# One inference step of a small RWKV-7 and pooling decoder: the prompt's group norm computed inside the sample stage, and TensorE's loops written out

## The chip, the cores and the metric

The kernel runs on one core of a Trainium2 chip. Its metric is the device time of that core in microseconds (us): the median of the runs shown. Five engines run their own instruction streams and meet at semaphores: PE (TensorE), DVE (VectorE), ACT (ScalarE), POOL (GpSimd) and SP (SyncE), which issues the DMAs. "PEld" in the profile is TensorE loading weights.

## What is computed

Two layers: RWKV-7 time mixing, then a pooling mixer, each followed by a feed-forward block. Both a prompt of 512 tokens and 8 sequences of 4 sample tokens go through them, all in float32. The part at issue is the end of the time mixing: the recurrence's output y is normalised within each head of 64 channels, gets a bonus, is gated and multiplied by `w_o`:

```python
S, y = wkv7_scan(wkv_prev, r_h, hd(decay), k_h, v_h, -kk, kk * a_h)
mu = jnp.mean(y, axis=-1, keepdims=True)
var = jnp.mean(jnp.square(y - mu), axis=-1, keepdims=True)
y = ((y - mu) * lax.rsqrt(var + GN_EPS)).reshape(B, T, D) * gn_w + gn_b
bonus = jnp.sum(r_h * k_h * r_k, axis=-1, keepdims=True) * v_h
g = jax.nn.sigmoid(xg @ g1) @ g2
out = ((y + bonus.reshape(B, T, D)) * g) @ w_o
x = x + out
h = rmsnorm(x, norm_ffn)
x = x + jnp.square(jax.nn.relu(h @ ffn_w1)) @ ffn_w2
```

## The kernel before

Activations lie with channels on partitions: 1024 channels are KT = 8 tiles of 128, and the free dimension holds T = 544 tokens, 512 of the prompt and 32 of the samples. `X` is the residual, `R` first r and then y, `V` first v and then the bonus, `GH` the hidden layer of the gate. The order of all work is written by hand. TensorE fills numbered "jobs"; job j writes PSUM banks 2(j mod 4) and 2(j mod 4)+1, so it waits until job j-4 has been emptied. ACT and DVE, each in its own written order, empty the jobs (`wait_filled`, `wait_emptied`).

The stages, in order: loading, the projections r, k, v, and then

- **tiles**: the prompt's recurrence in TILES = 4 tiles of 128 tokens. `pe_tile` (with `dve_tile`, `act_tile`, `pool_tile`) runs three times in a loop `Fori` on every engine and once more written out, as the last tile. A tile begins on TensorE with `Q0` to `Q3` (L655), which need the rates that DVE writes last (L1642), goes on with `M`, the products of the first square `P2` (L600), and ends with `YU` (L793).
- **sample stage** (`pe_samples`, `act_samples`, `dve_samples`): the 32 sample tokens. The states are transposed in (`s0t0` to `s0t3`, L561), then come `Q`, `M`, `P2`, `tBK`, `XT2`, `tV`, `bonus`, the 256 small products of `GY` (L879), `tG`, `U`, `YU`, and for four pairs of sequences the state sums `SS0` to `SS3` (L912, each added on DVE by L1798) and the transposes `TO0` to `TO3` (L561), whose copies SP stores.
- **group norm** for all 544 tokens, after the samples (`GN_JOBS`): for each of 8 tiles a `mean` (L1016, a product of 128 rows with `bmean`), one `var` (L1004: eight tiles summed into 16 rows), eight `gate` jobs (L1020 with 128 rows and L1021 with 32 rows of `g2`), and eight `spread` jobs (L1018: 16 rows of 1/std spread to 128 channels). Each job is two products of 272 columns. DVE subtracts the mean (L1950), takes the reciprocal (L1953), and then for each tile multiplies (L1960), adds the bonus (L1965) and gates (L1969); ACT makes the high part (L1383) and DVE the low part (L1972) of the result, which `w_o` needs.
- **w_o**: four units of weights of 256 columns, 384 products (L547), then the sums of squares of the norm (L575), and
- the first feed-forward block: CHUNKS = 4 passes of a loop on every engine (3072 products, L547); pooling; the second feed-forward block alike; the outputs.

A float32 product is two records in the trace; the large products are split into three products of a rounded type (`xs_hi`, `xs_lo`, `w_hi`, `w_lo`). `act_split` and `dve_split` make the two parts of a unit of weights, of which two buffers exist. The loops on TensorE are these, and the same `with` stands before both calls of `pe_ffn`:

```python
            with pe.Fori(0, TILES - 1) as i:
                pe_tile(pe, i)
            pe_tile(pe, TILES - 1, last=True)
```

## Time and profile before

| | |
|---|---|
| median of 3 runs (lowest to highest) | 1521.79 us (1521.44 to 1523.41) |
| the profiled execution | 1522.32 us, of which its span 1520.3 us |
| busy over the span: PE, PEld | 1438.9 us (95%), 1383.5 us (91%) |
| busy: DVE, ACT, POOL | 713.3 us (47%), 513.8 us (34%), 29.2 us (2%) |
| mean granted TensorE clock | 0.953 |
| DMA | 100.90 MB, 21.1% of the 16 engines' time on queue 1 |

The span runs from the first to the last instruction; a row's times are in it. "Busy" for PE is the union of modelled, overlapping products, so it says when PE had work, not how fast that work went. The granted clock is 1.00 at 2.4 GHz and 0.50 at 1.2 GHz. A group's mean covers one record; successive records overlap, so what a record costs in a row of them is the group's time over its count.

### The profile page before, as it was taken

Reading aid. Unit: us, or ns where it says so; the run is one execution under the profiler, and the core shown is the slowest. Engines: PE = TensorE matmul, PEld = TensorE weight load, DVE = VectorE, ACT = ScalarE, POOL = GpSimd, SP = SyncE. Lnnn points to the kernel's source line nnn. Section 1 sums busy time; section 2 is a strip of 40 time slices with the busy share of each in tenths; the row PEclk is TensorE's granted clock in tenths of the full one; section 3 lists DMA queues with packets and bytes.
Section 4 is the critical chain, followed back from the end, with each engine's and each line's share of the span. In section 5 each row is a group of like instructions: output and inputs, shape, how many; then the busy total and the mean of one; then the engine's idle time right before and its main releaser. Section 6 shows DMA issues by size and latency. Waiting matters only on the chain.

```text
span 1520.3 us, 33819 instructions
## 1 busy us (share of the span) xinstructions
PE 1438.9 (95%) x14990; PEld 1383.5 (91%) x14990; DVE 713.3 (47%) x859; ACT 513.8 (34%) x661; POOL 29.2 (2%) x28
## 2 busy tenths in 40 slices
PE   5899998898999889999999999999499999999998
PEld 4899998898989885899999999999389999999998
DVE  7746257585762423744334234343774233343332
ACT  5433236363543334333223132132153123131234
POOL 0000001010110000000000000000000000000000
PEclk7999999999999759799999999999799999999999
DMA  5123300000030014022222222221222322223211
GB/s 153 56 84 103 98 1 3 4 3 4 3 58 4 9 41 116 28 84 84 87 85 97 92 83 83 83 83 55 69 71 89 106 83 83 83 83 104 85 60 59
DMA packets 108887, 100.90 MB, mean 66 GB/s; under 512 B 21552, under 2 KB 106872, under 8 KB 108786
## 3 DMA queue, kind: packets, MB, share of 16 engines
q1 hardware_dynamic: 108786, 99.36, 21.1%
q8 instruction: 87, 1.43, 0.4%
q14 instruction: 14, 0.11, 0.0%
HBM read 94.18 MB, written 5.18 MB: 65 GB/s over the span
## 4 chain that ended last, share of the span: by engine, by line
PE 61%; DVE 3%; issue 1%; ACT 1%; DMA 0%; ACTq 0%; DVEq 0%
PE ps L547 54%; PE ps L575 1%; DVE pool_sum L2015 1%; PE ps L561 1%; PE ps L912 1%; PE ps L879 1%; PE ps L1021 1%; PE ps L1020 1%; PE ps L1016 1%; PE ps L1004 0%; DVE r_all L1965 0%; DVE r_all L1960 0%; DVE xs_lo L1972 0%; DMA pool_state_rows<-in_state_pool 0%; DVE pool_diff L2021 0%
## 5 line engine op out<-in xcount | busy, mean ns | idle before, releaser
L547 PE MATMUL ps<-xs_hi,w_hi 128*128 128x272 f32 (+1 forms) x2656 | 555.4, 290 | 16.6 <-DVE xs_lo L1904 8.6
L547 PE MATMUL ps<-xs_hi,w_lo 128*128 128x272 f32 (+1 forms) x2656 | 552.9, 290 | 0.0
L547 PE MATMUL ps<-xs_lo,w_hi 128*128 128x272 f32 (+1 forms) x2656 | 551.0, 289 | 0.0
L547 PEld LDWEIGHTS ps<-xs_hi,w_hi 128*128 128x128 f32 (+1 forms) x2656 | 420.0, 189 | 20.4 <-issue 11.1
L547 PEld LDWEIGHTS ps<-xs_lo,w_hi 128*128 128x128 f32 (+1 forms) x2656 | 419.5, 189 | 0.5
L547 PEld LDWEIGHTS ps<-xs_hi,w_lo 128*128 128x128 f32 (+1 forms) x2656 | 416.4, 189 | 0.5
L1471 DVE TENSOR_TENSOR w_lo<-w_raw,w_hi 128x2048 fp32r<-128x2048 f32 (+1 forms) x83 | 188.7, 2273 | 165.0 <-ACT w_hi L1122 164.4
L1122 ACT ACTIVATE w_hi<-w_raw 128x2048 fp32r<-128x2048 f32 (+1 forms) x83 | 157.0, 1891 | 291.4 <-PE ps L547 286.0
L1822 DVE TENSOR_TENSOR x_res<-x_res,ps 128x544 f32<-128x544 f32 x64 | 46.1, 720 | 207.4 <-PE ps L547 207.4
L1285 ACT ACTIVATE square_tmp<-relu_tmp 128x544 f32<-128x544 f32 x64 | 42.2, 659 | 268.1 <-DVE relu_tmp L1816 268.1
L1816 DVE SCALAR_TENSOR_TENSOR relu_tmp<-ps,rstd 128x544 f32<-128x544 f32 x64 | 46.3, 723 | 130.0 <-PE ps L547 130.0
L1828 DVE TENSOR_TENSOR xs_lo<-square_tmp,xs_hi 128x544 fp32r<-128x544 f32 x64 | 45.7, 725 | 71.3 <-ACT xs_hi L1293 71.3
L1293 ACT ACTIVATE xs_hi<-square_tmp 128x544 fp32r<-128x544 f32 x64 | 40.3, 642 | 0.0
L1664 DVE TENSOR_TENSOR wkv_FT_XT<-wkv_FT_XT,ps 128x512 f32<-128x512 f32 x32 | 21.7, 687 | 34.0 <-PE ps L600 33.8
L1046 PE MATMUL ps<-pool_diff,pool_w_whole 128*128 128x272 f32 x64 | 20.0, 478 | 15.9 <-DVE pool_diff L2022 11.4
L1046 PEld LDWEIGHTS ps<-pool_diff,pool_w_whole 128*128 128x128 f32 x64 | 14.8, 238 | 20.7 <-issue 12.2
L655 PE MATMUL ps<-rates_recept,b_k_hat 64*128 64x128 f32 x256 | 19.7, 322 | 8.6 <-issue 6.5
L655 PEld LDWEIGHTS ps<-rates_recept,b_k_hat 64*128 64x128 f32 x256 | 19.0, 235 | 9.2 <-issue 9.2
L1328 ACT ACTIVATE xs_hi<-xs_full 128x544 fp32r<-128x544 f32 x24 | 15.6, 654 | 29.5 <-DVE xs_full L1884 26.7
L1160 ACT ACTIVATE wkv_F<-ps 128x512 f32<-128x512 f32 x24 | 14.3, 597 | 20.7 <-PE ps L600 20.7
L2059 POOL TENSOR_TENSOR wkv_RBK<-wkv_RBK,const_sb 128x512 f32<-128x512 f32 x16 | 20.5, 1313 | 1.0 <-ACT wkv_RBK L1179 1.0
L773 PE MATMUL ps<-wkv_NV,wkv_FT_XT 64*64 64x64 f32 x256 | 16.4, 219 | 3.9 <-issue 2.4
(314 smaller groups left out, 1409.8 us busy)
## 6 DMA issues: line engine op xcount, KB each, us to landing
w_raw<-in_ffn_w SPq DMA_DIRECT2D x64, 1024.0 KB, 5.2
w_raw<-in_rwkv_w_rkv SPq DMA_DIRECT2D x12, 1024.0 KB, 5.2
w_raw<-in_rwkv_w_o SPq DMA_DIRECT2D x4, 1024.0 KB, 6.3
x_rows<-in_x_prompt SPq DMA_DIRECT2D x4, 512.0 KB, 5.8
smp_state_rows<-in_state_wkv SPq DMA_DIRECT2D x8, 256.0 KB, 5.9
...
```

The lines of the kernel that those rows point to most:

```text
L547: mm = nc.tensor.matmul(bank(j, h)[0:w, 0:TH], wt[:, kw, c0:c0 + w], xt[:, kx, h * TH:(h + 1) * TH], start=(begins and n == 0 and wt is wh ...
L655: mm = nc.tensor.matmul(bank(j, p)[:, cols], BKH[rows, gc].rearrange("p x n -> p (x n)"), AR[rows, gc].rearrange("p x n -> p (x n)"), star ...
L1046: mm = nc.tensor.matmul(bank(j, h)[:, 0:TH], WPL[:, k, c0:c0 + P], DF[:, k, h * TH:(h + 1) * TH], start=(k % 2 == 0), stop=(k % 2 == 1))
L1122: act(WHI[u % 2][:, :, 0:w], RAW[u % 2][:, :, 0:w], ACT.Copy).then_inc(whi_made, 1)
L1285: act(QL[:, m % 2, :], RL[:, m % 2, :], ACT.Square).then_inc(square_made, 1)
L1293: act(HH[:, m, :], QL[:, m % 2, :], ACT.Copy).then_inc(hhi_made, 1)
L1471: tt(WLO[b][:, :, 0:w], RAW[b][:, :, 0:w], WHI[b][:, :, 0:w].bitcast(F32), SUB).then_inc(wlo_made, 1)
L1664: tt(m3(XT_, h), m3(XT_, h), b3(name, h), ADD).then_inc(emptied[jw(i, name) % 4], 1)
L1816: stt(halves(RL[:, m % 2, :]), both(j, TH), 0.0, halves(RS1[:]), MAX, MUL)\
L1822: tt(halves(X[:, m - 8, :]), halves(X[:, m - 8, :]), both(j, TH), ADD).then_inc(emptied[j % 4], 2)
L1828: tt(HL[:, m, :], QL[:, m % 2, :], HH[:, m, :].bitcast(F32), SUB).then_inc(hlo_made, 1)
L2059: ins = mask(rows, rows, over(CC["UI"], KT), MUL)
```

## The change

The group norm of the prompt's 512 columns becomes jobs of the sample stage, and that of the 32 sample columns becomes small jobs of its own (`smean`, `svar`, `sspread`, `sgate`). A prompt job now covers two tiles of 512 columns, one in each bank: four `mean`, four `gate`, four `spread`, and one `var`. `var` sends its eight products to four groups of 32 output columns of the array (`bank(j, 0)[32 * c:32 * c + 32]`), and 1/std then lies in four groups of rows (partitions 0, 32, 64, 96), so that `head_spread` multiplies four rows of another row group for each tile, with a table `HRN` that eight small DMAs load. `GG` moves to another place of SBUF, `g2` is loaded after `apre`, the sample states move from the raw weight buffers to weight buffer 0 (with that, ACT's wait for KP before the first state copy goes), and the first unit of `w_o` is loaded and split within the stage. TensorE's three loops are written out; the other engines keep theirs. The core of the diff:

```diff
--- before.py
+++ after.py
-SMP_JOBS = ("wpre", "apre", "norm2", "s0t0", "s0t1", "s0t2", "s0t3", "Q", "M", "P2", "tBK", "XT2", "tV", "bonus", "GY",
-            "tG", "U", "YU", "SS0", "SS1", "TO0", "SS2", "TO1", "SS3", "TO2", "TO3")
+SMP_JOBS = ("wpre", "apre", "norm2", "s0t0", "s0t1", "s0t2", "s0t3", "sgate", "mean0", "Q", "M", "mean1", "P2", "mean2",
+            "tBK", "XT2", "tV", "mean3", "bonus", "var", "gate0", "GY", "tG", "U", "gate1", "YU", "SS0", "gate2",
+            "spread0", "smean", "SS1", "TO0", "gate3", "svar", "spread1", "SS2", "TO1", "sspread", "spread2", "SS3",
+            "TO2", "spread3", "TO3")
...
-J_GN = J_SMP + len(SMP_JOBS)
-GN_JOBS = ([("mean", k) for k in range(KT)] + [("gate", k) for k in range(4)] + [("var", 0)]
-           + [("gate", k) for k in range(4, KT)] + [("spread", k) for k in range(KT)])
-J_WO = J_GN + len(GN_JOBS)
+J_WO = J_SMP + len(SMP_JOBS)
...
-        S0T = at("smp_state", [P, NB // 2, KT, 2, HD], o_raw)
-        SO = at("smp_state_out", [P, NB // 2, D], ww(0))
+        S0T = [at(f"smp_state{q}", [P, KT, 2, HD], ww((0, 1, 4, 5)[q])) for q in range(NB // 2)]
+        SO = [at(f"smp_state_out{q}", [P, D], ww((0, 1, 4, 5)[q])) for q in range(NB // 2)]
...
-        G2A, G2B = at("g2_a", [P, D], o_a), at("g2_b", [LG - P, D], o_a + 4096)
-        GG = at("gn_gate", [P, KT, T], o_a + 8192)
-        GR = at("gn_rstd", [P, T], o_a + 8192 + FB)[HROWS]
+        G2A, G2B = at("g2_a", [P, D], slots[15]), at("g2_b", [LG - P, D], slots[16])
+        GR = at("gn_rstd", [P, T], o_s)
+        SGT = at("smp_gate", [P, KT, NS], o_s + 2560)
+        HRN = at("head_rows_by_group", [P, 2, P], o_l)
+        GQS = at("smp_squares", [P, KT, NS], o_l + 1024)
+        GG = at("gn_gate", [P, KT, T], o_b + FB)
...
+            wait_filled(sp, J_STO)
+            sp_unit(sp, U_WO, wo_v[:, :, 0:UW])
             wait_emptied(sp, J_STO)
             store(sp, o["wkv_prompt"][0, 0].rearrange("h v k -> v h k"), STO[:].rearrange("v (h k) -> v h k", k=HD))
-            wait_emptied(sp, js("GY"))
+            wait_filled(sp, js("apre"))
+            heads = a["head_rows"].rearrange("n (k p) -> n k p", k=KT)
+            for c in range(4):
+                for e in range(2):
+                    n = 2 * c + NH // 2 * e
+                    sp.dma_start(HRN[32 * c + 2 * e:32 * c + 2 * e + 2], heads[n:n + 2, c::4, :]).then_inc(headrow_loaded, 16)
             sp.dma_start(G2A[:], a["rwkv_g2"][0, 0:P]).then_inc(g2_loaded, 16)
             sp.dma_start(G2B[:], a["rwkv_g2"][0, P:LG]).then_inc(g2_loaded, 16)
+            sp.wait_ge(out_stored, 16 * stores[0])
+            sp_unit(sp, U_WO + 1, wo_v[:, :, UW:2 * UW])
...
+            def mean(m):
+                j = js(f"mean{m}")
+                wait_free(pe, j)
+                if m == 0:
+                    w_kept(pe, TILES - 1, "YU")
+                for e in range(2):
+                    mm = nc.tensor.matmul(bank(j, e), bmean, R[:, 2 * m + e, 0:SEQ], start=True, stop=True)
+                mm.then_inc(filled, 2)
+
+            def var(e):
+                j = js("var")
+                if e == 0:
+                    wait_free(pe, j)
+                pe.wait_ge(gn_squared, 2 * e + 2)
+                for c in range(4):
+                    mm = nc.tensor.matmul(bank(j, 0)[32 * c:32 * c + 32, :], CT[:, c0 - 2 * e:c0 - 2 * e + 32],
+                                          GQ[:, c + 4 * e, 0:SEQ], start=(e == 0), stop=(e == 1))
+                if e == 1:
+                    mm.then_inc(filled, 2)
+
+            def gate(m, parts=(0, 1)):
+                j = js(f"gate{m}")
+                if parts[0] == 0:
+                    wait_free(pe, j)
+                for e in parts:
+                    cols = slice((2 * m + e) * P, (2 * m + e + 1) * P)
+                    nc.tensor.matmul(bank(j, e), G2A[:, cols], GH[:, 0, 0:SEQ], start=True, stop=False)
+                    mm = nc.tensor.matmul(bank(j, e), G2B[:, cols], GH[0:LG - P, 1, 0:SEQ], start=False, stop=True)
+                if parts[-1] == 1:
+                    mm.then_inc(filled, 2)
+
+            def head_spread(m):
+                j = js(f"spread{m}")
+                wait_free(pe, j)
+                if m == 0:
+                    pe.wait_ge(headrow_loaded, 16 * 9)
+                    pe.wait_ge(gn_rstd, 1)
+                for e in range(2):
+                    k = 2 * m + e
+                    rows = slice(32 * (k % 4), 32 * (k % 4) + 4)
+                    mm = nc.tensor.matmul(bank(j, e), HRN[rows, k // 4, :], GR[rows, 0:SEQ], start=True, stop=True)
+                mm.then_inc(filled, 2)
+
+            def sample_mean():
...
+            sums(0)
+            gate(2)
+            head_spread(0)
+            sample_mean()
+            sums(1)
+            out_rows(0)
+            gate(3)
+            sample_var()
+            head_spread(1)
+            sums(2)
+            out_rows(1)
+            sample_spread()
+            head_spread(2)
+            sums(3)
+            out_rows(2)
+            head_spread(3)
...
-            with pe.Fori(0, TILES - 1) as i:
+            for i in range(TILES - 1):
...
-            with pe.Fori(0, CHUNKS) as i:
+            for i in range(CHUNKS):
...
-                if q == 0:
-                    s_dve(eng, "KP")
-                act_copy_out(eng, js(f"s0t{q}"), S0T[:, q].rearrange("p (e g) b v -> p e (g b v)", e=2), both(js(f"s0t{q}")))
+                act_copy_out(eng, js(f"s0t{q}"), S0T[q][:].rearrange("p (e g) b v -> p e (g b v)", e=2), both(js(f"s0t{q}")))
...
+            def high(k):
+                eng.wait_ge(gn_step, k + 1)
+                act(XSH[1][:, k, :], R[:, k, :], ACT.Copy).then_inc(gn_hi, 1)
+
+            masked_uv(0)
+            gate(1)
+            masked_uv(1)
+            gate(2)
+            masked_uv(2)
+            wait_emptied(eng, js("smean"))
+            act(GQS[:], R[:, :, SEQ:T], ACT.Square).then_inc(gn_squared, 1)
+            out_rows(0)
+            gate(3)
+            gn_root("svar", slice(SEQ, T))
+            masked_uv(3)
+            out_rows(1)
+            wait_filled(eng, js("SS3"))
+            eng.wait_ge(gn_smp, 4)
+            for k in range(4):
+                high(k)
+            out_rows(2)
+            for k in range(4, 6):
+                high(k)
+            out_rows(3)
+            for k in range(6, KT):
+                high(k)
 
...
+            def head_spread(m):
+                j = js(f"spread{m}")
+                ks = (2 * m, 2 * m + 1)
+                if m == 0:
+                    w_kept(eng, TILES - 1, "bonus")
+                wait_filled(eng, j)
+                for e, k in enumerate(ks):
+                    stt(R[:, k, 0:SEQ], R[:, k, 0:SEQ], col(GNW + k), bank(j, e), MUL, MUL).then_inc(emptied[j % 4], 1)
+                for e, k in enumerate(ks):
+                    wait_emptied(eng, j, e)
+                    stt(R[:, k, 0:SEQ], R[:, k, 0:SEQ], col(GNB + k), V[:, k, 0:SEQ], ADD, ADD).then_inc(gn_biased, 1)
+                wait_emptied(eng, js(f"gate{m}"))
+                for k in ks:
+                    eng.wait_ge(gn_biased, k + 1)
+                    tt(R[:, k, 0:SEQ], R[:, k, 0:SEQ], GG[:, k, 0:SEQ], MUL).then_inc(gn_step, 1)
+
+            def rstd(name, cols):
...
+            summed(0)
+            head_spread(0)
+            sample_mean()
+            summed(1)
+            sample_bias()
+            rstd("svar", slice(SEQ, T))
+            head_spread(1)
+            summed(2)
+            sample_spread()
+            head_spread(2)
+            summed(3)
+            head_spread(3)
 
         def dve_ffn(eng, l, i, last, norm=None):
...
             for k in range(KT):
-                j = jg("mean", k)
-                wait_filled(eng, j)
-                tt(halves(R[:, k, :]), halves(R[:, k, :]), both(j, TH), SUB).then_inc(emptied[j % 4], 2)
-            dve_split(eng, U_WO)
-            wait_emptied(eng, jg("var", 0))
-            nc.vector.reciprocal(GR[:], GR[:]).then_inc(gn_rstd, 1)
-            for n in range(KT + 2):
```

The places in the order of instructions on which the prediction rests. First TensorE at the end of a tile: `YU` (L793, then L802) and `Q0` of the next tile (L655, then L664). Before:

```order
L782 MATMUL ps<-wkv_UV,wkv_BKT 64x64 [waits psum_emptied0]
L782 MATMUL ps<-wkv_UV,wkv_BKT 64x64 x7
L793 MATMUL ps<-wkv_RBK,wkv_UV 64x64 [waits psum_emptied2,rbk_masked]
L793 MATMUL ps<-wkv_RBK,wkv_UV 64x64 x31
L989 REGISTER_ALU
L989 COMPARE_AND_BRANCH
L655 MATMUL ps<-rates_recept,b_k_hat 128x128 [waits dve_prep,psum_emptied3]
```

and with the change:

```order
L791 MATMUL ps<-wkv_UV,wkv_BKT 64x64 [waits psum_emptied0]
L791 MATMUL ps<-wkv_UV,wkv_BKT 64x64 x7
L802 MATMUL ps<-wkv_RBK,wkv_UV 64x64 [waits psum_emptied2,rbk_masked]
L802 MATMUL ps<-wkv_RBK,wkv_UV 64x64 x31
L664 MATMUL ps<-rates_recept,b_k_hat 128x128 [waits dve_prep,psum_emptied3]
L664 MATMUL ps<-rates_recept,b_k_hat 128x128 x7
```

The register step and the branch back are gone; the next tile's `Q0` follows `YU` in the stream.

Then TensorE from the samples' `YU` on (L900 before, L1004 with the change). Before, `SS0`, `SS1` (L912) and `TO0` (L561):

```order
L900 MATMUL ps<-smp_RBK,smp_UV 64x32 [waits psum_emptied0,psum_emptied1]
L900 MATMUL ps<-smp_RBK,smp_UV 64x32 x15
L912 MATMUL ps<-smp_uv_masked_161,smp_BKT 64x128 [waits smp_act_feature,psum_emptied2]
L912 MATMUL ps<-smp_uv_masked_161,smp_BKT 64x128 x15
L912 MATMUL ps<-smp_uv_masked_162,smp_BKT 64x128 [waits smp_act_feature,psum_emptied3]
L912 MATMUL ps<-smp_uv_masked_162,smp_BKT 64x128 x15
L561 MATMUL ps<-const_sb,smp_state 128x128 [waits psum_emptied0,psum_emptied2]
L561 MATMUL ps<-const_sb,smp_state 128x128 x7
```

and with the change, where L854 and L855 are `gate2`, L868 is `spread0` and L875 the samples' mean:

```order
L1016 MATMUL ps<-smp_uv_masked_161,smp_BKT 64x128 [waits smp_act_feature,psum_emptied2]
L1016 MATMUL ps<-smp_uv_masked_161,smp_BKT 64x128 x15
L854 MATMUL ps<-g_hidden,g_a 128x512 [waits psum_emptied3]
L855 MATMUL ps<-g_hidden,g_b 128x512
L854 MATMUL ps<-g_hidden,g_a 128x512
L855 MATMUL ps<-g_hidden,g_b 128x512
L868 MATMUL ps<-gn_rstd,head_rows_by_group 128x512 [waits gn_rstd,headrow_loaded,psum_emptied0]
L868 MATMUL ps<-gn_rstd,head_rows_by_group 128x512
L875 MATMUL ps<-r_all,const_sb 128x256 [waits psum_emptied1]
L1016 MATMUL ps<-smp_uv_masked_162,smp_BKT 64x128 [waits smp_act_feature,psum_emptied2]
L1016 MATMUL ps<-smp_uv_masked_162,smp_BKT 64x128 x15
```

Four gate products and the first two spreads now stand between the state sums; `gate0` and `var` stand in `GY`, `gate1` between `U` and `YU`, and the means between the jobs from `M` to `tV`.

Last DVE around the first state sum (L1798 before, L1983 with the change). Before, ending with the means of the group norm:

```order
L1791 TENSOR_TENSOR r_all<-r_all,ps 128x8x32 [waits psum_emptied2,psum_filled]
L1798 TENSOR_TENSOR smp_state<-smp_state,ps 128x512 [waits psum_filled,smp_dve_feature]
L1798 TENSOR_TENSOR smp_state<-smp_state,ps 128x512
L1798 TENSOR_TENSOR smp_state<-smp_state,ps 128x512 [waits psum_filled,smp_dve_feature]
L1798 TENSOR_TENSOR smp_state<-smp_state,ps 128x512
L1950 TENSOR_TENSOR r_all<-r_all,ps 128x544 [waits psum_filled] x8
L1471 TENSOR_TENSOR w_lo_60<-w_raw_56,w_hi_58 128x2048 [waits whi_made,raw_loaded1]
L1953 RECIPROCAL gn_rstd<-gn_rstd 16x544 [waits psum_emptied2]
L1960 SCALAR_TENSOR_TENSOR r_all<-r_all,params,ps 128x544 [waits psum_filled,psum_emptied1]
```

and with the change:

```order
L1991 TENSOR_TENSOR r_all<-r_all,ps 128x8x32 [waits psum_emptied1,psum_filled]
L1983 TENSOR_TENSOR smp_state_164<-smp_state_164,ps 128x512 [waits psum_filled,smp_dve_feature]
L1983 TENSOR_TENSOR smp_state_164<-smp_state_164,ps 128x512
L1885 SCALAR_TENSOR_TENSOR r_all<-r_all,params,ps 128x512 [waits psum_filled,psum_emptied1]
L1885 SCALAR_TENSOR_TENSOR r_all<-r_all,params,ps 128x512
L1888 SCALAR_TENSOR_TENSOR r_all<-r_all,params,v_all 128x512 [waits psum_emptied0] x2
L1892 TENSOR_TENSOR r_all<-r_all,gn_gate 128x512 [waits gn_biased,psum_emptied0]
L1892 TENSOR_TENSOR r_all<-r_all,gn_gate 128x512 [waits gn_biased]
L1902 TENSOR_TENSOR r_all<-r_all,ps 128x8x32 [waits psum_emptied1,psum_filled]
L1983 TENSOR_TENSOR smp_state_165<-smp_state_165,ps 128x512 [waits psum_filled,smp_dve_feature]
L1983 TENSOR_TENSOR smp_state_165<-smp_state_165,ps 128x512
L1913 TENSOR_TENSOR v_all<-v_all,params 128x8x32 [waits psum_emptied2]
```

Six operations on a pair of tiles (L1885, L1888, L1892) now stand before the second state sum; three more such sixes follow between and after the others.

## Rows read from the trace of the kernel before

**Rows 1.** The chain that ended last, share of the span by line.
```profile
by line: PE ps L547 53.6%; PE ps L575 1.1%; DVE pool_sum L2015 1.0%; PE ps L561 1.0%; PE ps L912 0.9%; issue 0.8%; PE ps L879 0.8%; PE ps L1021 0.7%; PE ps L1020 0.7%; PE ps L1016 0.5%; PE ps L1004 0.5%; DVE r_all L1965 0.4%; DVE r_all L196
```
**Rows 2.** The same chain in order of time: start us, us, what.
```profile
527.56 12.17 PE ps L879 x256
...
551.20 7.09 PE ps L912 x64
558.29 1.90 PE ps L561 x8
...
572.91 7.86 PE ps L1016 x32
...
591.02 7.44 PE ps L1004 x32
...
631.56 45.51 PE ps L547 x348
677.08 4.58 PE ps L575 x20
681.66 384.85 PE ps L547 x3072
```
**Rows 3.** Waits of PE: us in total, times, longest.
```profile
PE ps L655 <- issue: 6.5, 2, 3.3
```
**Rows 4.** Timeline at the three tile boundaries: start, us, engine, line, idle before.
```profile
301.69 3.78 PE L655 MATMUL ps<-rates_recept,b_k_hat 64*128 64x128 f32 x32 [3.34 <-issue]
...
312.09 2.08 PE L600 MATMUL ps<-wkv_P,wkv_P1T 64*64 64x64 f32 x64
...
372.71 3.99 PE L655 MATMUL ps<-rates_recept,b_k_hat 64*128 64x128 f32 x40 [3.18 <-issue]
...
382.30 2.08 PE L600 MATMUL ps<-wkv_P,wkv_P1T 64*64 64x64 f32 x64
...
438.59 1.28 DVE L1642 TENSOR_TENSOR rates_recept<-r_all,wkv_EL 128x512 f32<-128x512 f32 x2
...
440.02 3.84 PE L655 MATMUL ps<-rates_recept,b_k_hat 64*128 64x128 f32 x64 [0.29 <-DVE rates_recept L1642]
...
448.77 2.08 PE L600 MATMUL ps<-wkv_P,wkv_P1T 64*64 64x64 f32 x64
```
**Rows 5.** Windows: stretch, length, busy by engine, granted clock, DMA share, GB/s.
```profile
300.80:307.60 6.80, 5.91 (x55) 5.94 (x57) 3.44 (x7) 2.48 (x6) 0.00 (x0) 0.50 0.02 5
...
502.20:509.00 6.80, 6.80 (x31) 6.51 (x31) 5.16 (x10) 4.89 (x9) 0.00 (x0) 0.50 0.12 29
509.00:515.80 6.80, 2.84 (x74) 2.44 (x72) 5.00 (x14) 3.77 (x4) 0.00 (x0) 1.00 0.00 0
...
529.50:573.80 44.30, 40.20 (x429) 37.07 (x426) 10.86 (x15) 14.80 (x15) 0.00 (x0) 0.50 0.16 40
573.80:611.30 37.50, 37.50 (x141) 20.22 (x140) 13.28 (x13) 14.26 (x20) 0.00 (x0) 1.00 0.40 112
611.40:625.00 13.60, 13.60 (x42) 10.84 (x41) 13.36 (x20) 3.29 (x5) 0.00 (x0) 0.50 0.00 0
628.50:635.20 6.70, 5.37 (x22) 5.05 (x23) 5.43 (x7) 3.12 (x3) 0.00 (x0) 0.50 0.01 2
```
**Rows 6.** Groups by line and shape, PE, 220 to 632 us: busy us, mean ns.
```profile
L912 PE MATMUL ps<-smp_uv_masked,smp_BKT 64*64 64x128 f32 x128 | 14.4, 419 | 0.3 <-ACT smp_uv_masked L1260 0.3
...
L692 PE MATMUL ps<-wkv_Z,const_sb 128*128 128x512 f32 x16 | 7.7, 606 | 0.7 <-ACT wkv_RBK L1179 0.7
```
**Rows 7.** Timeline of the sample stage's first products, PE, and its first transposes.
```profile
499.07 1.87 PE L802 MATMUL ps<-w_hidden,w_aug 65*128 65x32 f32 x16
...
503.93 6.13 PE L561 MATMUL ps<-const_sb,smp_state_rows 128*128 128x128 f32 x32
```
**Rows 8.** Instructions on r_all: duration ns min/median/max, first and last start us.
```profile
L1734 DVE TENSOR_TENSOR r_all<-r_all,ps x8: 680/685/689, 298.5 to 499.0; 128x512 f32 x6, 128x512 f32<-128x512 f32 x2
...
L1960 DVE SCALAR_TENSOR_TENSOR r_all<-r_all,params,ps x8: 771/772/782, 609.5 to 626.6; 128x544 f32<-128x544 f32 x8
```

More of the change, by code:

```diff
@@ new lines, in sample_gate @@
+            def sample_gate():
+                j = js("sgate")
+                wait_free(pe, j)
+                pe.wait_ge(g2_loaded, 32)
+                for first in (True, False):
+                    for k in range(KT):
+                        w, rows = (G2A, slice(0, P)) if first else (G2B, slice(0, LG - P))
+                        mm = nc.tensor.matmul(bank(j, 0 if first else 1)[:, k * NS:(k + 1) * NS], w[rows, k * P:(k + 1) * P],
+                                              GH[rows, 0 if first else 1, SEQ:T], start=True, stop=True)
+                mm.then_inc(filled, 2)
@@ new lines, in sample_spread @@
+            def sample_spread():
+                j = js("sspread")
+                wait_free(pe, j)
+                pe.wait_ge(gn_rstd, 2)
+                for k in (0, 4, 1, 5, 2, 6, 3, 7):
+                    rows = slice(32 * (k % 4), 32 * (k % 4) + 4)
+                    mm = nc.tensor.matmul(bank(j, k % 2)[:, k // 2 * NS:(k // 2 + 1) * NS], HRN[rows, k // 4, :],
+                                          GR[rows, SEQ:T], start=True, stop=True)
+                    if k == 5:
+                        mm.then_inc(smp_spread_half, 1)
+                        pe.wait_ge(smp_spread_half, 1)
+                mm.then_inc(filled, 2)
@@ L1058, in run_pe @@
             pe_norm(pe, 3, J_N3)
-            with pe.Fori(0, CHUNKS) as i:
+            for i in range(CHUNKS):
                 pe_ffn(pe, 1, i)
@@ L1236, in act_samples, with squares, gn_root, gate @@
             for q in range(4):
-                if q == 0:
-                    s_dve(eng, "KP")
-                act_copy_out(eng, js(f"s0t{q}"), S0T[:, q].rearrange("p (e g) b v -> p e (g b v)", e=2), both(js(f"s0t{q}")))
+                act_copy_out(eng, js(f"s0t{q}"), S0T[q][:].rearrange("p (e g) b v -> p e (g b v)", e=2), both(js(f"s0t{q}")))
+            def squares(m):
+                wait_emptied(eng, js(f"mean{m}"))
+                act(GQ[:, 2 * m:2 * m + 2, 0:SEQ], R[:, 2 * m:2 * m + 2, 0:SEQ], ACT.Square).then_inc(gn_squared, 1)
+            def gn_root(name, cols):
+                j = js(name)
+                wait_filled(eng, j)
+                act(GR[:, cols], bank(j, 0)[:, 0:cols.stop - cols.start], ACT.Sqrt, bias=CC["eps"][:, 1:2],
+                    scale=1.0 / HD).then_inc(emptied[j % 4], 2)
+            def gate(m):
+                act_copy_out(eng, js(f"gate{m}"), GG[:, 2 * m:2 * m + 2, 0:SEQ], both(js(f"gate{m}")))
+            j = js("sgate")
+            wait_filled(eng, j)
+            act(SGT[:], s8(j), ACT.Copy).then_inc(emptied[j % 4], 1)
+            squares(0)
             rows2 = lambda T2: T2.rearrange("p (e n) -> p e n", e=2)
@@ L1366, in run_act @@
             act_samples(eng)
[L1368 to L1383 removed]
             for n in range(4):
+                if n == 0:
+                    eng.wait_ge(out_stored, 16 * (3 + NB))
                 act_split(eng, U_WO + n + 1)
@@ new lines, in sample_bias, with sample_spread @@
+            def sample_bias():
+                wait_emptied(eng, js("bonus"))
+                tt(V[:, :, tok], V[:, :, tok], spread(PRM[:, GNB:GNB + KT], NS), ADD).then_inc(gn_smp, 1)
+                eng.wait_ge(gn_squared, 5)
+                tt(R[:, :, tok], R[:, :, tok], spread(PRM[:, GNW:GNW + KT], NS), MUL).then_inc(gn_smp, 1)
+            def sample_spread():
+                j = js("sspread")
+                wait_filled(eng, j)
+                eng.wait_ge(gn_smp, 2)
+                for e in range(2):
+                    half = R[:, :, tok].rearrange("p (a e) n -> p e a n", e=2)[:, e]
+                    tt(half, half, bank(j, e)[:, 0:4 * NS].rearrange("p (a n) -> p a n", a=4), MUL)\
+                        .then_inc(emptied[j % 4], 1)
+                wait_emptied(eng, j)
+                tt(R[:, :, tok], R[:, :, tok], V[:, :, tok], ADD).then_inc(gn_smp, 1)
+                wait_emptied(eng, js("sgate"))
+                eng.wait_ge(gn_smp, 3)
+                tt(R[:, :, tok], R[:, :, tok], SGT[:], MUL).then_inc(gn_smp, 1)
@@ L1770, in dve_samples @@
             f(ins)
+            mean(1)
+            mean(2)
             need("XT1")
```

169 lines of the change are left out of this document (80 added, 89 removed).

## The prediction

> **What bounds the kernel now.** I read the chain of waits first. By line it is TensorE: the large products alone are 53.6% of the span [rows 1]. In order of time it shows where the change works: the group norm begins at 572.91 us, the unbroken run of `w_o` products at 631.56, the first feed-forward block at 681.66 [rows 2]. That block is one piece of 3072 products in 384.85 us, 0.1253 us each, with no gap where its loop turns. In the waits of PE one row belongs to a loop: L655, the first product of a tile, waited twice on nothing the profile shows, 6.5 us together [rows 3]. The windows show the third thing: the granted clock is 0.50 from 529.5 to 573.8 and 1.00 while the group norm's means, gates and variance run [rows 5]. So three things can change the time: the pauses at the loop's turns, the work between the samples and `w_o`, and the clock at which moved work runs. The chain's own execution took 1522.3 us, 2.0 outside its span and 0.5 above the median of 1521.8; I sum against 1522.3.
>
> **TensorE's loops.** At the two turns of the tile loop `Q0` starts 3.34 and 3.18 us after TensorE could have had it; at the third boundary, which is written out already, it starts 0.29 us after DVE's rates (438.59 + 1.28 = 439.87, start 440.02) [rows 4]. After the first turn the clock is at 0.50 for 6.8 us [rows 5], and from `Q0` to `P2` pass 10.40 and 9.59 us against 8.75 [rows 4]. Written out, each boundary should look like the third: (3.34 + 3.18 - 2 x 0.29) + (10.40 - 8.75) + (9.59 - 8.75) = 5.9 + 2.5 = **8.4 us** saved. The feed-forward loops give nothing: their turns are covered by the products still queued, as the unbroken piece shows. The longer stream is fetched at the pace at which straight code is now, and the last tile shows no pause of that kind, so I cost it at nothing; a rival takes the contrary.
>
> **What is removed behind the samples.** From 572.91 to the end of `w_o` (677.08) pass 104.2 us [rows 2]; the 384 products of `w_o` need 384 x 0.1253 = 48.1 of them, and half speed around 628.5 to 635.2 costs 2.9 (5.8 us of products at half rate) [rows 5]. I keep both. Removed are 104.2 - 48.1 - 2.9 = **53.2 us**.
>
> **What is added within the samples**, TensorE's path first:
>
> (a) Up to `GY`. `sgate`: 16 products of 32 columns, 32 records; 16 such records took 1.87 us [rows 7], so 3.7 at least. It waits for `g2`, which SP issues behind eight small loads; I expect it about 1.5 us after the state transposes, about where ACT's now dropped wait for KP let `Q` begin. A `mean` job is two products of 512 columns; 16 records of that shape at clock 1.00 are 7.7 us, four are 1.9 [rows 6], 3.5 at half clock. One of the four hides behind DVE's work between `M` and `P2`. `GY` must find the bank of `mean3` emptied by DVE (two tiles, 2 x 0.69 [rows 8]). Sum: 3.7 + 3 x 1.9 to 3.5 + 1.4, less overlaps: 8 to 14, taken **10**.
>
> (b) In `GY` (12.17 us for its 256 records [rows 2]). Four gate jobs of 272 columns took 591.02 - 580.77 = 10.25 us [rows 2], 1.28 for a tile's half; at 512 columns 2.1 to 2.4 for a tile at clock 1.00, 3.9 at 0.50. `gate0` is 4.2 or 7.8. `var` is eight products, 16 records of 0.44 us at full clock (0.2325 x 512/272 [rows 2]), 7.0 us one after the other, 14 at half clock. That column groups work side by side the trace shows for halves: L912's 128 records of 128 columns cost 14.4/128 = 0.113 us at clock 0.50 [rows 6, 5], while a single stream needs 2 x 128/1.2 GHz = 0.213. Four groups have no row: between none and four times I take four less something, as the pair reached 1.9 of 2: 1.9 to 4.3. The small products leave the clock low, so mostly half speed: **11.5**, bounds 5.9 and 21. By the Trainium skill ("TensorE: Matmul & The Clock Gate", Part 3), three column tiles gave 2.38 times and four row tiles 3.07 times; at 3 times `var` would be 2.3 to 4.7 us and the sum the same within 1.
>
> (c) From `GY`'s end to `SS0` are 551.20 - 539.73 = 11.5 us [rows 2]; `gate1` adds 4.2 to 7.8, less about 1 us of ACT's copy of `U`, which it covers: **6**, bounds 3 and 6.8.
>
> (d) From `SS0` to the last transposes are 572.91 - 551.20 = 21.7 us, all at 0.50 [rows 2, 5]. Added: `gate2`, `gate3` (8.4 or 15.6), four spreads (two products of two row groups side by side; L655 does this at 3.84/64 = 0.060 us a record against 0.107 [rows 4], so 1.0 or 1.9 each), the samples' three jobs (2 to 3.4). That is 14 at full clock, 27 at half. If the gates lift the clock, the old 21.7 also shrink, eight transposes from 1.90 [rows 2] toward 1.06 and the sums with them, by up to 10. I take **18**, bounds 4 and 27. DVE has 4 x (2 x 0.69 + 6 x 0.73), 23 us, and some small ones of its own there [rows 8], less than TensorE's 40, and sets the floor.
>
> (e) Tail: after `spread3` come six operations on DVE (4.3 us) and the first high and low part, 1.3; TensorE's `TO3` covers 1.9. **3**, bounds 2 and 5.
>
> Removed too: DVE and ACT work of the old group norm lies beside; its eight low parts stay, as fast as TensorE eats them. `w_o`'s second unit waits until the stores of `TO3` have landed, and is split after that; the first unit runs 96 x 0.1253 = 12 us, and that is the cover: if stores and splitting take longer, TensorE waits there for the rest.
>
> Added: 10 + 11.5 + 6 + 18 + 3 = 48.5. Sum: 1522.3 - 8.4 - 53.2 + 48.5 = 1509.2, at the median **1509 us**.
>
> **Rivals.**
> - *Full clock* (20%). The interleaved 512-column work keeps 1.00 for most of the stage; added falls to about 29 (DVE's floor in (d)). Time 1522 - 61.6 + 29 = **1490**. For it: the clock rose at 573.8, within 1 us of the means' start [rows 5]. Against it: `GY` and the sums fill little of the array.
> - *Half clock throughout* (13%), the case on the slow side. From `sgate` to `w_o`'s first products the clock stays at 0.50: (a) 14, (b) 14.6 with `var` at 6.8, (c) 6.6, (d) 27, (e) 3, and 3.5 more at the start of `w_o`: 68.7. Time 1522.3 - 61.6 + 68.7 = **1529**. It is slower from 64.6 added on. For it: from 529.5 to 573.8 TensorE was busy 40.2 of 44.3 us and the clock never rose [rows 5]; four rows of a row group are less work still, and with 16 rows the clock fell at 611.4 [rows 5]. Against it: it rose at 509.0 after the state transposes [rows 5, 7]. The same page of the Trainium skill (Part 4) says that transposes do not count as activity for the clock; by that the `TO` jobs would not help and this rival would be the result. This trace disagrees: before 509.0 TensorE had done almost nothing but transposes (503.93 to 510.06) [rows 7], and the clock was granted.
> - *The pauses stay* (12%). If the 3.3 us were not the jump but the stream, straight code could pause as well, or the rates come late: 8.4 is not saved, time **1517**. Against it is the third boundary.
> - Between these, within 0.2% of before (1519 to 1525), 10%.
>
> **How the numbers follow.** Forecast 45%, own range 1502 to 1516, from +-7 in (b) and (d). The range for 8 in 10 reaches up into the half-clock case and down toward the full-clock one: **1493 to 1525**. What this kernel's runs can tell from no change is about 0.2%, 3 us. Faster: 45 + 20 + 12, less 1 that the third rival could lose: 76%. Within: 11%. Slower: 13%.
>
> **What would show it.** Tile boundaries with `Q0` within 0.5 us of DVE's rates and the clock 1.00 behind them. In the sample stage `var`'s 16 records in 2 to 4.5 us; a spread's four in 1 to 2. A gate job in 4.2 or 7.8 us, which tells the clock. `GY` starting 38 us after the stage's first transposes, `SS0` about 81 after it (53 before), the first `w_o` product at about 123 (133 before, but with 36 products ahead of it, and slow). The feed-forward blocks again 384.9 us each. Wrong would be: pauses in the written-out feed-forward, a wait of `w_o` for its second unit, or DVE as what ends TensorE's waits in the last third of the stage.

## The result and the profile after

| kernel | median of runs, us | lowest to highest | ratio to before (95% interval) |
|---|---|---|---|
| before | 1521.8 (7 runs) | 1520.2 to 1524.5 | |
| changed | **1516.2** (7 runs) | 1512.7 to 1518.2 | 0.9960 (0.9948 to 0.9973) |

The change saves 5.6 us where 12.8 were forecast. The time lies in the wide forecast range (1493 to 1525) and just above the narrow one (1502 to 1516), and the direction was right; less than half of the gain came. The profiled execution of the changed kernel is the fastest of its seven (1512.7 us, span 1510.9), so what follows on the trace is 3.5 us better than the median and 9.6 below the profiled execution of before. The gain lies wholly in the tiles. First the waits of PE (us in total, times, longest), to be set against [rows 3], then its timeline at the first two boundaries and at `P2` (L609) behind each, against [rows 4].

```profile
PE ps L664 <- issue: 1.8, 1, 1.8
...
PE ps L664 <- DVE rates_recept L1763: 0.9, 3, 0.3
```
```profile
297.63 1.61 PE L664 MATMUL ps<-rates_recept,b_k_hat 64*128 64x128 f32 x24 [0.29 <-DVE rates_recept L1763]
...
306.30 1.91 PE L609 MATMUL ps<-wkv_P,wkv_P1T 64*64 64x64 f32 x58
...
363.59 1.61 PE L664 MATMUL ps<-rates_recept,b_k_hat 64*128 64x128 f32 x24 [0.29 <-DVE rates_recept L1763]
...
372.26 1.91 PE L609 MATMUL ps<-wkv_P,wkv_P1T 64*64 64x64 f32 x58
```

`Q0` (L664 now) starts 0.29 us behind DVE's rates at every boundary (the one wait on nothing left, 1.8 us, is not at a turn), and from `Q0` to `P2` pass 8.67 us at both turns, for 10.40 and 9.59. From the first of these `Q0` to the second pass 65.96 us where there were 71.0, and to the third 131.6 where there were 138.3 [rows 4]. The sample stage's first state transposes (L570) begin at 488.07; before they began at 498.17, 10.1 us later. Of these, 1.0 lies ahead of the first of these `Q0`, beyond its pause. The first feed-forward block begins at 672.14 (681.66 before [rows 2]), 9.5 earlier. So the sample stage with the group norm in it and `w_o` took 184.1 us, and 183.5 before: the move, forecast to save 4.7 us, cost 0.6 here. The chain in time of that stretch, with the parts that the prediction priced (start, us, what):

```profile
488.07 0.99 PE ps L570 x8
...
499.86 3.57 DMA g_b<-in_rwkv_g
...
503.56 5.84 PE ps L895 x32
...
529.41 1.12 PE ps L970 x32
...
532.55 1.86 PE ps L843 x8
...
539.90 2.00 PE ps L854 x2
...
572.75 3.47 PE ps L1016 x32
...
592.60 1.49 PE ps L854 x2
...
617.70 22.42 PE ps L556 x165
```
Read it as a list of prices. `sgate` (L895) is released by the landing of `g_b`, which SP issued behind its eight small loads (0.61 to 0.76 us each, the first at 493.60), and takes 5.84 us for 32 records. `var` (L843) takes 1.86 us for four products. One matrix of a gate (L854 or L855, two records) takes 2.00 us, so a gate job 8.0, until `gate3` at 592.60. The windows say why (stretch, length, busy by engine, granted clock):

```profile
505.00:515.20 10.20, 10.20 (x67) 7.42 (x68) 1.77 (x3) 1.11 (x2) 0.00 (x0) 0.50 0.06 22
515.20:532.30 17.10, 14.63 (x229) 10.40 (x224) 12.05 (x22) 7.81 (x8) 0.00 (x0) 1.00 0.01 2
532.30:593.70 61.40, 58.92 (x392) 33.04 (x388) 16.58 (x21) 15.20 (x16) 0.00 (x0) 0.50 0.00 1
593.70:600.50 6.80, 6.80 (x60) 3.24 (x60) 1.93 (x4) 3.18 (x5) 0.00 (x0) 1.00 0.37 80
600.60:621.00 20.40, 17.46 (x94) 13.35 (x93) 17.66 (x31) 8.06 (x13) 0.00 (x0) 0.50 0.42 88
```
From inside `GY` to `TO0` TensorE ran at 0.50 for 61.4 us and was busy for 58.9 of them. Before, the group norm's part had 37.5 us at 1.00 [rows 5]; the products moved from there into a stretch at half the clock. That the stretch behind the waiting (505.0 to 515.2) is at 0.50 too will matter below.

### The profile page after: what moved, and what is told of

It reads as the page before. It is cut to its first block, busy times and chain, and to the rows that moved or that the text cites. A ratio compares the mean times of both kernels' runs of the same rounds, so it can differ in the third digit from the quotient of the medians.

```text
span 1510.9 us, 33550 instructions
## 1 busy us (share of the span) xinstructions
PE 1433.0 (95%) x14976; PEld 1363.5 (90%) x14976; DVE 713.1 (47%) x864; ACT 511.6 (34%) x656; POOL 29.3 (2%) x28
## 3 DMA queue, kind: packets, MB, share of 16 engines
q1 hardware_dynamic: 108834, 99.39, 21.3%
## 4 chain that ended last, share of the span: by engine, by line
PE 90%; DVE 5%; issue 2%; ACT 1%; DMA 1%; SPq 1%; ACTq 0%; DVEq 0%
PE ps L556 66%; PE ps L609 6%; PE ps L584 1%; PE ps L782 1%; PE ps L693 1%; PE ps L570 1%; PE ps L854 1%; PE ps L791 1%; PE ps L622 1%; DVE pool_sum L2197 1%; PE ps L855 1%; PE ps L734 1%; PE ps L978 1%; PE ps L1016 1%; PE ps L834 1%
## 5 line engine op out<-in xcount | busy, mean ns | idle before, releaser
L1134 PEld LDWEIGHTS ps<-pool_diff,pool_w_whole 128*128 128x128 f32 x64 | 14.1, 226 | 20.9 <-issue 12.7
L782 PEld LDWEIGHTS ps<-wkv_NV,wkv_FT_XT 64*64 64x64 f32 x256 | 15.6, 135 | 5.1 <-issue 5.1
L609 PE MATMUL ps<-wkv_FT_XT,wkv_F 64*64 64x64 f32 x512 | 18.1, 219 | 0.2
```

What stands on the lines that cost most here:

```text
L609: mm = nc.tensor.matmul(bank(j, h)[rows, g * HD:(g + 1) * HD], L[rows, h, g, :], rhs, start=True, stop=True)
L782: mm = nc.tensor.matmul(bank(j, p)[0:HD, g * HD:(g + 1) * HD], FX[rows, p, g, 1, :], WT["NV"][rows, p, g, :], start=True, stop=True)
L1134: mm = nc.tensor.matmul(bank(j, h)[:, 0:TH], WPL[:, k, c0:c0 + P], DF[:, k, h * TH:(h + 1) * TH], start=(k % 2 == 0), stop=(k % 2 == 1))
```

## The experiments

All medians are in us, of five or more runs (e5 has two). A ratio is to runs of the kernel before made beside it on the same chip: e1 to e4 and e9 to e11 ran on one chip, e5 to e8 on another, e12 on a third.

| run | what it is | median | ratio to before (95%) |
|---|---|---|---|
| e1 | before, tile loop written out | 1513.8 | 0.9937 (0.9919 to 0.9955) |
| e2 | before, all three loops written out | 1513.7 | 0.9938 (0.9920 to 0.9956) |
| e3 | changed, feed-forward loops rolled up | 1537.8 | 1.0103 (1.0082 to 1.0125) |
| e4 | changed, all three loops rolled up | 1542.8 | 1.0133 (1.0113 to 1.0154) |
| e5 | before and 24 idle instructions | 1541.3 | 1.0113 (1.0077 to 1.0150) |
| e6 | e3 and 40 idle instructions | 1515.4 | 0.9950 (0.9931 to 0.9970) |
| e7 | changed, `g2` loaded first | 1506.4 | 0.9888 (0.9866 to 0.9910) |
| e8 | e7, means, `var`, two gates ahead of `GY` | **1496.4** | 0.9819 (0.9797 to 0.9841) |
| e9 | changed, once more | 1515.2 | 0.9966 (0.9949 to 0.9984) |
| e10 | e8, three gates ahead of `GY` | 1500.6 | 0.9850 (0.9825 to 0.9875) |
| e11 | e8, four gates ahead of `GY` | 1497.1 | 0.9838 (0.9815 to 0.9861) |
| e12 | e8, `mean1` to `mean3` later | 1503.9 | 0.9888 (0.9859 to 0.9917) |

### The loops: e1 to e4

```
e1, e2   - with pe.Fori(0, TILES - 1) as i:        + for i in range(TILES - 1):
e2       - with pe.Fori(0, CHUNKS) as i:           + for i in range(CHUNKS):      (both feed-forwards; the tile loop as in e1)
e3       + with pe.Fori(0, CHUNKS) as i:   in the changed kernel, both feed-forwards
e4       e3 and + with pe.Fori(0, TILES - 1) as i:
```
Expected of e1: 

> The kernel before, with TensorE's loop over the tiles alone written out; feed-forward loops and group norm as before. Theory L (the whole gain of the change is this loop, the moved group norm gives nothing): 8 to 10 us below the kernel before, so about 1512 to 1514, and below the changed kernel or level with it; the boundaries show Q0 within 0.5 us of DVE's rates and no low clock in the tiles. Rival M (the moved group norm carries half of the gain or more): 1517 to 1520. Rival F (the written-out feed-forward loops give some of the loop's gain back): this one is at 1512 to 1514 too, but the kernel with all three loops written out is 2 us or more above it.

Expected of e2: 

> The kernel before, with all three of TensorE's loops written out. Theory L: within 1 us of the kernel with the tile loop alone written out, about 1513, feed-forward blocks 384.9 us each. Rival F: 2 to 5 us above that one. Rival M: 1517 to 1520, like that one.

Expected of e3: 

> The changed kernel with its two feed-forward loops rolled up again, tile loop still written out, group norm still moved. Theory L: within 1 us of the changed kernel (1516). Rival F: 2 to 5 us below it (1511 to 1514).

Expected of e4: 

> The changed kernel with all three of TensorE's loops rolled up again: the moved group norm alone against the kernel before. Theory L: the move gives nothing or costs a little, 1521 to 1526, with the pauses of 3.2 us at the two turns of the tile loop back. Rival M: 1514 to 1518. By my prediction's sum (removed 53.2, added 48.5) it would be 1517.

The tile loop alone gave 8.3 us (1522.1 beside it to 1513.8); the sum had 8.4. In the kernel before, writing out the feed-forward loops as well gives 0.1. Up to here theory L holds. But e3 lies 21.6 us **above** the changed kernel, where I expected at most a few us in either direction. The chain of e3 in its first feed-forward shows three breaks, one for each jump back (the first stands here); with the loop written out it is one piece of 384.85 us:

```profile
674.28 96.21 PE ps L556 x768
770.49 1.91 issue
772.40 0.61 PE ps L556 x3
773.01 2.02 issue
775.03 98.44 PE ps L556 x765
```
A break is 4.5 to 5.2 us, and the 765 products behind one take 1.8 to 2.6 us more than at full clock (765 x 0.1253 = 95.9). The block ends 404.45 us after its start instead of 384.85, 19.6 us late. e3's second feed-forward is unbroken (3072 products in 384.85 us). In e4 it is the other way round: the first is one piece, the second is broken.

```profile
683.52 384.85 PE ps L556 x3072
...
1123.17 96.22 PE ps L556 x768
...
1221.65 2.84 issue
1224.49 98.61 PE ps L556 x767
```
The same loop, word for word, pays or does not. The record of TensorE's sequencer in the traces has the jump itself (COMPARE_BRANCH, ns):

```
                 tile loop     first feed-forward    second feed-forward
before           3804, 3646    242, 222, 207         223, 208, 207
e1               (none)        238, 213, 212         209, 207, 207
e3               (none)        3732, 3908, 3653      237, 222, 207
e4               3817, 3660    242, 222, 207         3724, 3387, 3753
```
There are two prices, 0.2 us and about 3.7 us (3.4 to 3.9), and nothing between. What differs is how many instructions stand ahead of the loop.

### Where a loop stands: e5 and e6

I counted TensorE's instructions in the compiled programs. The feed-forward's loop is 1569 of them, the tile loop 3004; TensorE's records in the traces, counted, give the same lengths within 2 and the same places within 4, once the 45 or so instructions ahead of the first record are added. Modulo 256, the feed-forward loops begin at 174 and 233 (before), 226 and 29 (e1), 195 and 254 (e3), 143 and 202 (e4). Those at 195 and 202 pay. Two kernels move the loops and do nothing else; two of the added waits make one instruction.

```
e5 (before):   + for _ in range(48):  pe.wait_ge(gsig_made, 2)     ahead of the tiles
e6 (e3):       + for _ in range(80):  pe.wait_ge(gsig_made, 2)     ahead of the tiles
```
Expected of e5 (the median of two runs, 1538.5 and 1544.1): 

> The kernel before with 48 waits that are already met on TensorE ahead of the tile loop: 24 more instructions, nothing else. Theory P (a jump back costs 0.2 us or 3.7 us by where the loop's first instruction stands in TensorE's stream, in blocks of 256; of the loops seen, those that begin at 195 and 202 of their block pay and those at 29, 143, 174, 226, 233, 254 don't): the first feed-forward loop moves from 174 to 198 and pays now, its three jumps 3.6 to 3.9 us each and about 20 us in all; the second moves from 233 to 1 and does not pay; time 1541 to 1544. Rival R (it depends on something else in the changed kernel, such as what its other queues do): 1522 to 1524, jumps 0.2 us.

Expected of e6: 

> The changed kernel with its feed-forward loops rolled up and 80 waits that are already met on TensorE ahead of the tiles: 40 more instructions. Theory P: the first feed-forward loop moves from 195 to 235 of its block and the second from 254 to 38, neither pays, jumps 0.2 us; time 1515 to 1519, 20 us less than the same kernel without these waits. Rival R: 1537 to 1540, as without them.

Both came as theory P says: e5 1541.3, e6 1515.4. The kernel before is 17.5 us slower than its runs beside it (1523.8) for 24 instructions that do nothing. Its chain breaks at the first jump of the first feed-forward, whose jumps are now 3353, 3585 and 3680 ns, and the second block stays whole:

```profile
679.74 96.22 PE ps L547 x768
775.96 1.53 issue
...
777.97 2.24 issue
```
```profile
1137.66 384.87 PE ps L547 x3072
```
In e6 both are whole, with jumps of 242 ns and less. Over all these kernels the loops at 195, 198 and 202 pay, and those at 1, 29, 38, 143, 174, 226, 233, 235 and 254 do not. The Trainium skill ("Runtime: NRT & Kernel Launch", Instruction fetch mechanics) gives a reason of this shape: TensorE's instruction memory holds 2048 instructions and is refilled in blocks of 256, and a jump whose target is not in the window that is held waits for its fetch. The same section calls that window two blocks, by which every jump over 1569 instructions would wait; most took 0.2 us here, so the trace does not agree with that part. By the 2048, 1569 instructions span seven blocks from most places and eight from a stretch of 32, the tile loop's 3004 span more than are held from anywhere, and the observed places fit if something from 30 to 49 instructions long stands ahead of the program; that last part is my estimate, and no run here measures what is held.

What the runs settle is this: **the moved group norm, with the loops rolled up, would have met a loss of 20 us that has nothing to do with it.** Against e2, with all loops out in both, the move costs 1516.2 - 1513.7 = 2.5 us by the medians (e9: 1.5); the intervals of the two ratios overlap, so a cost is not shown, but the gain of 4.7 is out. With e4, 1542.8 less the 20.5 us by which its second block is late, 1522.3 against 1522.1 before, it is 0.2. My sum had the move at -4.7 (added 48.5, removed 53.2).

### The load of g2: e7 and e9

```
  wait_filled(sp, js("apre"))
+ sp.dma_start(G2A[:], ...); sp.dma_start(G2B[:], ...)
  for c in range(4): for e in range(2): sp.dma_start(HRN[...], ...)        eight small loads
- sp.dma_start(G2A[:], ...); sp.dma_start(G2B[:], ...)
```
Expected of e7: 

> The changed kernel with the two loads of g2 issued ahead of the eight small loads of the head rows, instead of behind them. If the samples' gate waits for g2 because of that queue, its wait of 3.7 us goes and the stage is 3 to 4 us shorter: 1512 to 1513. If something else is late there (SMP features of DVE or the clock), it is 1515 to 1517.

Expected of e9: 

> The changed kernel once more, unchanged, on the chip and among the runs of the two below: 1514 to 1518. It says whether the 10 us between it and the run with g2 first, measured on another chip, are real (then it stays at 0.996 of the kernel before) or whether part of them is the chip (then it is nearer 0.993).

e7 is at 1506.4, 9 us under the changed kernel's 1515.2 in e9 (and its 1516.2 at first): more than twice the 3.7 us of the wait, and 6 below what was expected. e9 repeats the first ratio, but on another chip than e7's. What rules the chip out is e6: it has the changed kernel's sample stage, ran on e7's chip beside the same runs of before, and is at 1515.4. First e9's chain and TensorE's wait for `g2`, then e7's chain:

```profile
489.54 0.99 PE ps L570 x8
...
500.78 3.63 DMA g_b<-in_rwkv_g
...
504.55 7.14 PE ps L895 x32
```
```profile
PE ps L895 <- DMA g_b<-in_rwkv_g: 3.2, 1, 3.2
```
```profile
488.34 0.99 PE ps L570 x8
...
498.44 4.32 PE ps L895 x32
...
522.76 1.12 PE ps L970 x32
...
611.15 28.95 PE ps L556 x218
```
Seen from the stage's first transposes, `sgate` starts at 15.0 us in e9 and at 10.1 in e7, and then takes 7.14 against 4.32. That is 7.7 us by the end of `sgate`, of which e9's wait is 3.2. The windows (e9's three, then e7's two) show the rest. In e9 the clock is at 0.50 for 6.8 us ahead of the wait, where e7 has 1.00, and for 13.6 us behind it, where e7 has 6.8.

```profile
493.40:500.20 6.80, 6.80 (x31) 6.51 (x31) 5.03 (x9) 6.13 (x11) 0.00 (x0) 0.50 0.42 123
500.20:503.70 3.50, 1.16 (x11) 0.92 (x9) 2.28 (x7) 2.50 (x3) 0.00 (x0) 0.99 0.70 224
503.70:517.30 13.60, 12.75 (x72) 9.99 (x73) 1.64 (x2) 0.92 (x2) 0.00 (x0) 0.50 0.20 69
```
```profile
488.30:498.40 10.10, 8.53 (x75) 8.19 (x74) 6.89 (x13) 8.04 (x12) 0.00 (x0) 1.00 0.64 197
...
501.80:508.60 6.80, 6.80 (x57) 4.08 (x58) 1.82 (x3) 1.15 (x2) 0.00 (x0) 0.51 0.37 131
```
The stretch ahead of the wait is not the load's doing, for e8, with `g2` first, has it too (0.53 from 494.4 to 501.3). But the sum does not hang on it: in the five profiled executions with `g2` behind the small loads (changed, e3, e4, e6, e9) `sgate` ends 21.3 to 22.6 us after the first transposes, in the five with `g2` first (e7, e8, e10 to e12) 14.1 to 15.4. The other 1.2 us between the profiled executions of e9 and e7 lie ahead of the stage (489.54 and 488.34).

### Where the gates stand: e8, e10, e11

The order of the jobs is what changes; every engine's list is written to match. ACT's split of `w_o`'s first unit moves too, from ahead of `mean3`'s squares to behind the copies of the gates that stand ahead of `GY`; no run separates that from the jobs.

```
e7:  ... sgate mean0 Q M mean1 P2 mean2 tBK XT2 tV mean3 bonus var gate0 GY tG U gate1 YU SS0 gate2 spread0 ... TO0 gate3 svar ...
e8:  ... sgate mean0 mean1 Q M mean2 P2 mean3 tBK XT2 tV var gate0 bonus gate1 GY tG U gate2 YU SS0 spread0 ... TO0 gate3 svar ...
e10: ... var gate0 bonus gate1 gate2 GY tG U gate3 YU SS0 spread0 ... TO0 svar ...
e11: ... var gate0 bonus gate1 gate2 gate3 GY tG U YU SS0 spread0 ... TO0 svar ...
```
(In e7 `var` and `gate0` stand inside `GY`.)

Expected of e8: 

> g2 first as in the run before, and the means one place earlier each, var and gate0 and gate1 ahead of GY rather than inside it and behind U, gate2 behind U rather than behind SS0. Theory C (these products are dear where the granted clock is 0.50, and it is 1.00 between the means): gate0 and gate1 take 4.2 to 4.6 us instead of 8.0, 7 us below the run with g2 first alone, about 1505. Rival H (the clock falls with the small products wherever the dense ones stand, or DVE's and ACT's chain is what these jobs covered): 1510 to 1514.

Expected of e10: 

> As the run with gate0 and gate1 ahead of GY, with gate2 there too and gate3 behind U (TO0 has none behind it). Theory C (place of the clock): gate2 takes 4.2 us instead of 8.0 and one gate of 7.7 us leaves the half-clock stretch: 3 to 4 us below that run, about 1493. Rival H: 1496 or above.

Expected of e11: 

> All four gates ahead of GY and none behind U. Theory C: gate3 takes 4.2 us instead of 8.0, less 1 us of ACT's copy of U that it covered: 2 to 3 us below the run with three, about 1490. Rival H: level with it or above, because TensorE then waits for ACT behind U and for the four gates' copies ahead of GY.

e8 is 10 us below e7, where 7 would have been theory C's (it comes to 1496.4 for the 1505 expected), and 27.5 below the kernel before beside it (1523.8), the lowest median of this study; it beats both kernels of the case. Its chain and windows are as theory C has them: `gate0` and `gate1` take 1.05 us for two records where they took 2.00, the second half of `var` 1.07 where it took 1.86, and the clock is at 1.00 until `GY` has begun. `gate2`, behind `U`, still takes 2.0.

```profile
522.92 1.07 PE ps L843 x8
523.99 1.05 PE ps L854 x2
...
554.68 2.01 PE ps L854 x2
```
```profile
501.30:535.40 34.10, 31.87 (x321) 18.99 (x319) 13.53 (x29) 14.72 (x16) 0.00 (x0) 0.99 0.10 32
535.40:613.90 78.50, 73.08 (x541) 51.13 (x540) 40.91 (x58) 24.47 (x29) 0.00 (x0) 0.50 0.17 41
```
e10 and e11 have three and four gates there. In the profiled executions the stretch from the first transposes to `w_o`'s first product shrinks as expected: 117.5 us (e8), 114.6 (e10), 111.1 (e11), 122.8 in e7. The medians do not follow: 1496.4, 1500.6, 1497.1, with intervals that overlap. The runs of e8 fall in two groups, five from 1495.8 to 1497.6 with a mean granted clock of 0.960 or 0.961 and two at 1502.1 and 1504.2 with 0.954; the profiled one is the 1504.2. So the same program differs by 8 us with the clock it is granted, and the profile of e8 is not that of its median. By the medians e10 is on rival H's side (1496 or above) and not at theory C's 1493, and e11 is 3.5 us below e10, as C had it, but level with e8 and 7 above the 1490 expected. In the traces the gates cost what C says (1.05 us for two records ahead of `GY`). Whether three or four gates ahead of `GY` are worth more than two stays open.

### One step too far: e12

```
e8:  sgate mean0 mean1 Q M mean2 P2 mean3 tBK          e12:  sgate mean0 Q M mean1 P2 mean2 mean3 tBK
```
Expected of e12: 

> The run with gate0 and gate1 ahead of GY, with mean1 back between M and P2 and mean2 and mean3 together behind P2. In that run TensorE waited 4.5 us before P2 (509.3 to 513.7), because DVE took off the second pair of means (1.22 us) ahead of P2's operands; the changed kernel waited 0.6 there. If that is DVE's order, 1.2 of mean1 and part of the wait go to work that TensorE has anyway, and the stage is 2 to 3 us shorter: 1493 to 1495. If var then waits as long for ACT's squares, it is level, 1496 to 1498.

Wrong: 1503.9, and from 1497.6 to 1513.8. The expectation rested on a misread chain. In e8 the chain goes over DVE from 509.3 to 513.7, but that is not a wait of TensorE: it ran `Q`, `M` and `mean2` meanwhile and sat idle for 0.84 us of it. e12 has the same 0.84, so there was nothing to win there. What did change is `var`'s wait for ACT's squares, two in a row now, 2.33 us for 1.39 (the timeline of e8, then that of e12, then e12's chain and window):

```profile
513.74 1.17 PE L824 MATMUL ps<-smp_P,smp_P1T 32*32 32x32 f32 x32 [0.84 <-DVE smp_RBK L1942]
...
522.92 1.07 PE L843 MATMUL ps<-gn_squares,const_sb 128*32 128x512 f32 x8 [1.39 <-ACT gn_squares L1328]
```
```profile
510.12 1.17 PE L824 MATMUL ps<-smp_P,smp_P1T 32*32 32x32 f32 x32 [0.84 <-DVE smp_RBK L1941]
...
521.97 1.48 PE L843 MATMUL ps<-gn_squares,const_sb 128*32 128x512 f32 x8 [2.33 <-ACT gn_squares L1328]
```
```profile
519.92 2.01 ACT gn_squares L1328 x2
```
```profile
522.80:526.20 3.40, 3.40 (x8) 1.00 (x4) 0.00 (x0) 1.97 (x2) 0.00 (x0) 0.54 0.00 0
```
Behind that wait the clock is at 0.54 for 3.4 us, where `gate0` stands. From the first transposes to the first product behind `gate1` pass 45.2 us in e12's profiled execution and 42.6 in e8's; from there to `w_o` it is 68.4 against 74.9, as the clock came back to 0.98 for 6.8 us (577.4 to 584.2) in e12 and not in e8. The six runs of e12 have mean clocks from 0.959 (1497.6 us) to 0.948 (1513.8). Whether `var`'s wait is what spreads them was not tried.

## Why the prediction was right and wrong

- **TensorE's loops, 8.4 us: right to 0.1** (e1), by the mechanism and the size of the two boundaries: the trace of the changed kernel has 5.9 us less of pauses and 1.7 + 0.9 less from `Q0` to `P2`. The rival that the pauses stay is out.
- **"The feed-forward loops give nothing: their turns are covered by the products still queued": right in the kernel before, wrong as a reason.** They are covered because those jumps cost 0.2 us there, not because any jump would be. At 3.7 us the queue does not cover them, as the tile loop had shown me [rows 3], and e5 makes it so in the kernel before. In the changed kernel the loops rolled up would cost 22 us. That the third part of the change was worth anything was in no case of mine.
- **The step that failed is the work added within the samples, and in it (a), up to `GY`.** I took 10 us for (a) and it was 13.1 (`GY` at 41.3 us into the stage, 28.2 before). I let `g2` land about 1.5 us behind the transposes and cost `sgate` at 3.7; it waited 3.7 and then took 5.84, in e9 3.2 and 7.14. That SP issues `g2` behind eight small loads I had seen and not priced: eight at 0.65 us are 5.2, ahead of a transfer of 3.6. The clock behind the wait I had not thought of. With `g2` first `GY` starts at 34.4, so the term is 6.2, 6.9 less.
- **The other terms**, in the profiled execution: (b) 11.5 forecast, 12.3 measured (`GY` 529.41 to 554.96, less the 13.3 of before); `var` 3.7, within its 2 to 4.5, so four column groups do run side by side; `gate0` 8.0, its dear value. (c) 6 and 6.3. (d) 18 and 20.4, `gate2` at 8.0, `gate3` at 4.65 in a short return of the clock, each `spread` 1.0 to 2.0. (e) 3 and 2.8, though its own figures, 4.3 + 1.3 - 1.9, give 3.7; the bounds of (b) should have been 6.1 and 21.8. Added are 54.9, where the sum had 48.5 and removed were 53.2; `w_o` itself took 49.9 for 51.0. In e7 the stage up to `w_o` is 122.8 us, against the 123 of my forecast and 129.6 in the changed kernel: had `g2` come first, the forecast would have been 3 us off (1506.4 to 1509). That would have been luck in part: (a) would have been 3.8 too high and (b), (c) and (d) together 3.5 too low.
- **The wait of `w_o` for its second unit** did not occur: 384 products in one piece of 49.86 us. Nor did DVE end TensorE's waits in the last third of the stage: the chain there is TensorE's own up to `spread3`.
- **The rival of half clock throughout** came close in the place I gave it: 61.4 us at 0.50 in one piece. Its 1529 was not reached because three of the means, `gate3` and most of `w_o` had the full clock. The rival of full clock is out as the change stands. Part of it can be had by the order of jobs: the added work is 54.9 us in the changed kernel, 48.1 in e7 and 42.8 in e8's profiled execution, where the rival had 29.

So the forecast was short by 6.4 us in the added work, 3.1 of it in (a) behind one load's place in a queue and 2.4 in (d); `w_o` gave 1.1 of it back. The medians miss the 4.7 us of the move by 7.2, of which this trace shows 5.3; the other 1.9 are not located, and the execution traced is 3.5 us faster than the median. And the forecast was right by luck on a loop's jump that it did not know.
